# Recurrence of a hybrid transformer step: GpSimd's identity copy moved in the period, and three parts of the output weights instead of one among the last unit's steps

## What is computed

```python
def step(s, inp):
    r_t, w_t, k_t, v_t, z_t, b_t = inp
    sz = jnp.einsum('bhvk,bhk->bhv', s, z_t)
    s = s * w_t[:, :, None, :] + sz[..., None] * b_t[:, :, None, :] + v_t[..., None] * k_t[:, :, None, :]
    return s, jnp.einsum('bhvk,bhk->bhv', s, r_t)
...
o = ((o - mu) * lax.rsqrt(var + GN_EPS)).reshape(bsz, t_len, C_W)
o = o * lp['ln_g'] + lp['ln_b'] + (bonus_f + bonus_b).reshape(bsz, t_len, C_W)
g = jax.nn.sigmoid(xg) @ lp['g_lora']
return o * g, s_f, s_b
...
y = jnp.concatenate([y_a, y_b, y_c], axis=-1) @ lp['w_out']
x = x + g1 * y
```

## Time and profile before

| | |
|---|---|
| median of 3 runs | 2250.51 us (2247.64 to 2252.56) |
| profiled execution, its own time | 2250.14 us |
| its span on the core | 2248.3 us |
| mean granted TensorE clock | 0.968 |
| busy: PE, DVE, ACT, POOL | 93%, 47%, 33%, 7% |
| recurrence (start of its first period to ZU of the last unit) | about 635 to 955 us |
| output projection, block 0, parts 1 to 7 | 978 to 1008 us |

### The profile page before, as it was taken

How to read it: one execution, slowest core, us unless ns; L and a number is a source line. 1 busy time by engine, 2 the same in 40 slices (tenths; PEclk the granted TensorE clock), 3 DMA queues, 4 the chain that set the end, 5 groups by cost and what they waited for, 6 DMA issues and landing times.

```text
span 2248.3 us, 43915 instructions
## 1 busy us (share of the span) xinstructions
PE 2091.7 (93%) x19377; PEld 1834.2 (82%) x19377; DVE 1065.4 (47%) x1850; ACT 748.2 (33%) x1230; POOL 155.0 (7%) x248
## 2 busy tenths in 40 slices
PE   5899999999878888789799999999999999999997
PEld 2688888777657776678699999999999998887886
DVE  1432225554647777644554434444444444445444
ACT  2231222222454444422343233333232333333433
POOL 1000000000224433300000000000000000000000
PEclk8899999999889999989999999999999999999999
DMA  9888777775410010063343344334433446333441
GB/s 388 320 279 299 259 278 282 274 258 199 82 30 9 11 30 4 25 243 131 118 144 120 125 131 131 121 124 131 131 122 122 131 132 233 124 130 113 131 129 59
DMA packets 195999, 343.01 MB, mean 153 GB/s; under 512 B 14253, under 2 KB 137827, under 8 KB 193696
## 3 DMA queue, kind: packets, MB, share of 16 engines
q1 hardware_dynamic: 194416, 335.14, 43.8%
q0 software_dynamic: 1392, 5.05, 0.8%
HBM read 332.62 MB, written 10.31 MB: 153 GB/s over the span
## 4 chain that ended last, share of the span: by engine, by line
PE 81%; DVE 6%; POOL 4%; issue 4%; DMA 2%; ACT 2%; POOLq 0%; DVEq 0%; ACTq 0%; SPq 0%
PE ps L753 24%; PE ps L754 24%; PE ps L755 24%; PE ps L787 4%; DMA ring<-in_w_mod_dram 2%; POOL arena L716 1%; POOL ring L716 1%; POOL arena L733 1%; POOL w_mix L643 1%; POOL u_buf L732 1%; PE ps L985 0%; PE ps L995 0%; PE ps L977 0%; PE ps L979 0%; DVE h_split L1651 0%
## 5 line engine op out<-in xcount | busy, mean ns | idle before, releaser
L1589 DVE TENSOR_TENSOR w_split<-ring,w_split 128x1024 fp32r<-128x1024 f32 (+1 forms) x392 | 475.4, 1219 | 733.2 <-ACT w_split L1266 732.8
L1266 ACT ACTIVATE w_split<-ring 128x1024 fp32r<-128x1024 f32 (+1 forms) x392 | 407.0, 1051 | 827.5 <-PE ps L755 581.3
L753 PE MATMUL ps<-h_split,w_split 128*128 128x384 f32 x1776 | 599.3, 337 | 10.4 <-DVE w_split L1589 6.4
L755 PE MATMUL ps<-h_split,w_split 128*128 128x384 f32 x1776 | 595.9, 336 | 0.0
L754 PE MATMUL ps<-h_split,w_split 128*128 128x384 f32 x1776 | 595.9, 336 | 0.0
L753 PEld LDWEIGHTS ps<-h_split,w_split 128*128 128x128 f32 x1776 | 335.3, 189 | 23.8 <-issue 15.9
L754 PEld LDWEIGHTS ps<-h_split,w_split 128*128 128x128 f32 x1776 | 335.3, 189 | 0.0
L755 PEld LDWEIGHTS ps<-h_split,w_split 128*128 128x128 f32 x1776 | 335.2, 189 | 0.0
L753 PE MATMUL ps<-w_split,h_split 128*128 128x512 f32 (+1 forms) x528 | 199.5, 378 | 3.4 <-DVE w_split L1589 3.4
L754 PE MATMUL ps<-w_split,h_split 128*128 128x512 f32 (+1 forms) x528 | 196.4, 372 | 0.0
L755 PE MATMUL ps<-w_split,h_split 128*128 128x512 f32 (+1 forms) x528 | 196.3, 372 | 0.0
(11 more groups left out here) (373 smaller groups left out, 2623.6 us busy)
## 6 DMA issues: line engine op xcount, KB each, us to landing
ring<-in_w_mod_dram SPq DMA_DIRECT2D x96, 1024.0 KB, 8.1
ring<-in_w_up_dram SPq DMA_DIRECT2D x88, 1024.0 KB, 5.1
ring<-in_w_in_dram SPq DMA_DIRECT2D x46, 1024.0 KB, 5.6
ring<-in_w_down_dram SPq DMA_DIRECT2D x44, 1024.0 KB, 5.4
ring<-in_w_out_dram SPq DMA_DIRECT2D x16, 1024.0 KB, 5.2
arena<-in_x_sample_dram SPq DMA_DIRECT2D x4, 1024.0 KB, 14.3
x_mid<-arena SPq DMA_DIRECT2D x1, 3072.0 KB, 10.2
h_f<-x_mid SPq DMA_DIRECT2D x1, 3072.0 KB, 11.3
```

What stands on the lines that cost most here:

```text
L753: mm(o_, lh, rh, start=start, stop=False)
L755: return mm(o_, ll, rh, start=False, stop=stop)
L1266: AC(wh[k % SPLITS][:, 0:width(n)], arrived(n), ACT.Copy).then_inc(s_hi, 1)
L1589: V.tensor_tensor(wl[k % SPLITS][:, 0:w], arrived(n), wh[k % SPLITS][:, 0:w].bitcast(F32), ALU.subtract).then_inc(s_lo, 1)
```

## The change

It moves two steps, moves three rows of parameters, and takes parts 1 and 2 of the output projection's first block forward. TTp goes to the front of GpSimd's period, behind the square roots. eT becomes a step of its own behind X2's copy on ACT. Rows 9 to 11 of group 2 are loaded into `par[1]`, after group 1's last normalization. Parts 0 to 2 are split on ACT and DVE in periods 18 and 19, and their nine tiles are multiplied at fixed places among PE's steps.

```diff
-ORDER_ACT = ["ZU", "X0", "tanh", "X1", "eW", "exps", "X2", "X3", "out", "AV", "tr", "X4", "F2"]
+ORDER_ACT = ["ZU", "X0", "tanh", "X1", "eW", "exps", "X2", "eT", "X3", "out", "AV", "tr", "X4", "F2"]
-ORDER_POOL = ["F0", "kk", "k0", "bon", "Bb", "dP", "TTp"]
+ORDER_POOL = ["F0", "kk", "k0", "TTp", "bon", "Bb", "dP"]
...
+        def closing(gr):
+            return min(gr, 1)
...
+                    b = gr % 2 if i < 9 else closing(gr)
...
-                    for i in range(4):
+                    for i in range(3):
                         if i:
                             sp.wait_ge(s_rlora, NG + 3 + i)
                         params(2, range(3 * i, 3 * i + 3))
+                if gr == 1:
+                    sp.wait_ge(s_fy, 6)
+                    sp.wait_ge(s_fg, 6)
+                    params(2, range(9, 12))
...
-            def out_part(j, p):
+            def out_tile(j, p, t):
                 n = P_OUT + OUT_PARTS * j + p
                 pe.wait_ge(s_lo, rank(n) + 1)
...
+                if j == 0 and p == OUT_PARTS - 1:
+                    pe.wait_ge(s_fc, 3 * GROUPS)
...
+            early_tiles = {(NU, "QMms"): [(0, 0)], (NU, "S0"): [(0, 1)], (NU, "S1"): [(0, 2)], (NU, "F2"): [(1, 0), (1, 1), (1, 2)],
+                           (NU + 1, "F1"): [(2, 0)], (NU + 1, "F2"): [(2, 1), (2, 2)]}
             for u in PERIODS:
-                if u == NU + 1:
-                    pe.wait_ge(s_rdone, NU - 1)
-                    out_part(0, 0)
-                for step in steps(ORDER_PE, u):
-                    rwkv_step(u, *step)
-            pe.wait_ge(s_fc, 3 * GROUPS)
+                for step, v in steps(ORDER_PE, u):
+                    rwkv_step(u, step, v)
+                    for p, t in early_tiles.get((u, step), ()):
+                        if p == t == 0:
+                            pe.wait_ge(s_rdone, NU - 1)
+                        out_tile(0, p, t)
...
     ACT:
+                    if step == ("ZU", NU - 1):
+                        ac.wait_ge(s_rTu, LEVELS * NU)
+                        hi(P_OUT + 1)
+                        ac.wait_ge(s_rbp, NU)
+                        hi(P_OUT + 2)
...
-                if n == P_OUT + 1:
-                    ac.wait_ge(s_fc, 3 * GROUPS)
-                if n > P_OUT:
+                if n == P_OUT + 3:
+                    ac.wait_ge(s_fy, 3 * GROUPS)
+                if n > P_OUT + 2:
                     hi(n)
...
     DVE:
-                    if u == NU and step[0] == "F1a":
-                        lo(P_OUT)
+                    if (u, step[0]) in ((NU, "F1a"), (NU, "O"), (NU + 1, "F1a")):
+                        lo(P_OUT + ((NU, "F1a"), (NU, "O"), (NU + 1, "F1a")).index((u, step[0])))
```

More of the change, by code:

```diff
@@ L518, in params @@
             def params(gr, rows=range(12)):
-                cs, b = slice(HW * gr, HW * gr + HW), gr % 2
+                cs = slice(HW * gr, HW * gr + HW)
                 src = [a["rwkv_w0"][0, 0:1, cs], a["rwkv_w0"][0, 1:2, cs], a["rwkv_a0"][0, 0:1, cs], a["rwkv_a0"][0, 1:2, cs],
@@ L1140, in rwkv_step @@
                 elif step == "F1":
-                    pe.wait_ge(s_parf[pb], 16 * 3 * (gr // 2 + 1))
+                    pe.wait_ge(s_parf[closing(gr)], 16 * 3 * (1 + gr // 2))
                     if FINAL[v % NG][0]:
@@ L1146, in rwkv_step @@
                         pe.wait_ge(s_S0, 2 * gr + 2)
-                    mm(ps[:, 7, 0:HW], lora[:, 2, toks(FINAL[v % NG][1])], par[pb][:, 11, :], start=True, stop=True).then_inc(s_fg, 1)
+                    mm(ps[:, 7, 0:HW], lora[:, 2, toks(FINAL[v % NG][1])], par[closing(gr)][:, 11, :], start=True, stop=True).then_inc(s_fg, 1)
                 elif step == "F2":
@@ L1158, in out_part @@
                 w_hi, w_lo = parts(n, OUT_KQ)
-                for t in range(3):
[L1160 to L1166, removed]
-            for u in PERIODS:
-                if u == NU + 1:
-                    pe.wait_ge(s_rdone, NU - 1)
-                    out_part(0, 0)
-                for step in steps(ORDER_PE, u):
-                    rwkv_step(u, *step)
-            pe.wait_ge(s_fc, 3 * GROUPS)
+                if j >= 2 and p == 0:
+                    pe.wait_ge(s_oc, 3 * (j - 2) + t + 1)
+                if j == 0 and p == OUT_PARTS - 1:
+                    pe.wait_ge(s_fc, 3 * GROUPS)
+                for k in range(OUT_KQ):
+                    q = OUT_KQ * p + k
+                    last = three(ps[:, 3 * (j % 2) + t, 0:OUT_W], yh[:, q, toks(t)], yl[:, q, toks(t)],
+                                 w_hi[:, k, :], w_lo[:, k, :], start=(q == 0), stop=(q == KT - 1))
+                if t == 2:
+                    last.then_inc(s_blk, 1)
+            def out_part(j, p):
+                for t in range(3):
+                    out_tile(j, p, t)
+            early_tiles = {(NU, "QMms"): [(0, 0)], (NU, "S0"): [(0, 1)], (NU, "S1"): [(0, 2)], (NU, "F2"): [(1, 0), (1, 1), (1, 2)],
+                           (NU + 1, "F1"): [(2, 0)], (NU + 1, "F2"): [(2, 1), (2, 2)]}
+            for u in PERIODS:
+                for step, v in steps(ORDER_PE, u):
[4 more added lines that the diff above has]
+                        out_tile(0, p, t)
             pe.wait_ge(s_cyh, 1)
             for j in range(N_OUT):
-                for p in range(0 if j else 1, OUT_PARTS):
+                for p in range(0 if j else 3, OUT_PARTS):
                     out_part(j, p)
@@ L1421, in rwkv_step @@
                     AC(eN[z], ps[:, 2, 0:HW], ACT.Exp, scale=DECAY / 2, bias=expb[:, 4 + d:5 + d]).then_inc(s_rexp, 1)
+                elif step == "eT":
                     for c in range(2):
@@ L1940, in rwkv_step @@
                     elif step == "F1b":
-                        dv.wait_ge(s_parf[pb], 16 * 3 * (gr // 2 + 1))
-                        link(V.tensor_tensor(O, O, par[pb][:, 9, :], ALU.mult))
-                        link(V.tensor_tensor(O, O, par[pb][:, 10, :], ALU.add))
+                        dv.wait_ge(s_parf[closing(gr)], 16 * 3 * (1 + gr // 2))
+                        link(V.tensor_tensor(O, O, par[closing(gr)][:, 9, :], ALU.mult))
+                        link(V.tensor_tensor(O, O, par[closing(gr)][:, 10, :], ALU.add))
                         link(V.tensor_tensor(O, O, sq[1], ALU.add))
```

## The result

| | before | changed |
|---|---|---|
| median of the runs | 2248.21 us (5 runs, 2241.49 to 2252.56) | 2228.56 us (5 runs, 2225.95 to 2231.45) |
| profiled execution, its own time | 2250.14 us | 2228.56 us |
| its span | 2248.3 us | 2226.7 us |
| mean granted clock | 0.968 | 0.973 |

The ratio is 0.9914, with a 95% interval of 0.9899 to 0.9929: about 19.3 us less. The forecast was 2235.0 with a range of 2229.5 to 2243.5. The three runs before that the forecast started from were high: their median was 2250.51, that of the five runs here is 2248.21, and that of 18 runs beside the first experiments 2247.52.

A forecast was written before the change was run, and what follows sets the result against it. A chain of dependent steps was taken to bound the recurrence, and a full PE the projection from 982 on. Terms 8.8 - 0.1 + 6.7 = 15.4 us off 2250.14 gave 2235 us, range 2229.5 to 2243.5.

The forecast's parts named there:

- T0i's waits: Recurrence: GpSimd's identity copy ended twelve of 18 waits of T0i; moving it early leaves A as releaser, gaining 8.8 us.
- The forecast's sign: At T0i in the recurrence: all its waits would be released by PE line 1107 and none by the copy.
- so I charge nothing: Recurrence: the 0.40 us copy now runs where DVE works, but the square root still goes ahead of it; cost 0.
- eT and the start: ACT, first period: A(0) comes 1.9 us later, a table load (1.3) and part of X2's wait (0.5) go; +0.1 us.
- The handover: Recurrence to output projection: early tiles and splits remove PE's hole and the second low clock stretch; 6.7 us gained.
- +3.45: Handover: last transposes F2 start at 977.35 instead of 973.91, 3.45 us later on the chain.
- PE's instruction supply: Rival: unexplained PE gaps at fixed times eat the recurrence's gain, leaving 0 there; 2243.4 us, chance 0.10.
- The port decides: Rival: in seven normalization periods the copy meets DVE and costs its 0.40 us each, 2.8 us; 2237.5 us, chance 0.07.
- The clock stays low: Rival, handover: all nine tiles run at the low clock and parts 3 to 7 end 2 us later; 2243.4 us, chance 0.09.
- slower: Rival: low clock through the handover and on into parts 3 to 7; 2262 us with all 90 matmuls, chance 0.03.
- the copy was not the last: Rival: T0i's twelve waits were on A's matmuls all along, first term 0; above 2252 or 2249 us, chance 0.04.
- More than forecast: Rival, handover: the clock does not fall at 951.5 or rises by 962, up to 4 us more; 2231 us, chance 0.07.

The follow-up runs named there:

- E4: Changed kernel with the bonus's products back ahead of the identity copy on GpSimd, copy still ahead of Bb and dP; ratio 0.9944.
- E14: Same code as E4 again, side by side with the changed kernel; ratio 0.9930, median 2233.55 us.
- E12: Changed kernel with the identity copy ahead of the square root too, as GpSimd's first step of a period; ratio 0.9922, median 2230.05 us.
- E3: Changed kernel with the old GpSimd order and eT back ahead of X2's copy, so only handover and parameters changed; ratio 0.9962, 8.5 us less.
- E5: Changed kernel with the convolution's output back behind eT in the first period; ratio 0.9901.
- E11: The changed kernel measured once more, unaltered, in a later session; ratio 0.9916, median 2230.78 us.
- E1: Kernel before with one edit, GpSimd's identity copy moved ahead of the bonus; ratio 0.9964, 8.1 us less.
- E6: Changed kernel with all three tiles of part 0 behind S1, none before S0; ratio 0.9943.
- E8: Changed kernel with the convolution's output behind the copies of the first transposes on ACT; ratio 0.9887.
- E10: Changed kernel with part 0's first tile still before S0 and the other two behind S1; ratio 0.9929.
- E13: Same code as E8 again, beside the changed kernel on one chip; ratio 0.9895, median 2224.77 us.

## Why the prediction was right or wrong

- **T0i's waits** (8.8 us): the mechanism was right. The copy ends none of them any more, and the length of A's path is what they left. The twelve now start 0.10 to 0.11 us after A and not 0.05, so they gave 8.1 us. E4 and E14, with the copy early, eT moved and the bonus in its old place beside DVE, show it by itself: T0i(1) to T0i(17) takes 262.8 us as their mean and 271.0 in the two kernels with the old orders, 8.2 us. The forecast's sign, line 1107 as the releaser of all, is not what the view says: it gives line 1107 for five of the 18 and DVE's own line 1893 for the rest.
- **"so I charge nothing"** for the copy beside DVE: this step failed. The neighbour matters and the sign is opposite to the rival's: the copy didn't add 0.40 us, it took the place of a longer product. The rival spoke of it ("the copy would only take its place") and didn't price it. The saving is 0.35 us in seven periods at line 1939 (now 1961) and in two more at line 1788, 3.1 us in all (E4, E14, and E12 by its rows). With the waits that makes 11.2 us; the means of T0i(1) to T0i(17) are 271.0 us for the old orders (two profiles) and 259.9 for the changed code (seven), 11.1 apart. Line 1944, whose spread the forecast read for this, stands beside Bb's product (732), which the change left where it was; the line to read was 1939. The Trainium skill ("SBUF — State Buffer", section "SBUF: two separate sides") has the pair of ports locked for a whole instruction, and by that the order of the lengths was to be had in advance: the trace agrees in the order, with 0.27 and 0.28 us from GpSimd's end to DVE's. That is less than the 0.41 us that DVE's product takes alone.
- **eT and the start** (+0.1): wrong by a term. Where the clock's low stretches are alike it costs 0.8 to 0.9 us. The loss of A(0) was 3.0 us where 1.9 stood, because the copies of the transposes now start only after the second table load and eT. In the first pair of profiles it was hidden by the low stretch of 10 us in the kernel before.
- **The handover** (6.7): the mechanism was right, the term mis-sized: 8.4 us in the first pair of profiles and 8.5 us in E3 by its time. From F2(17) to part 8 it takes 23.8 us, which is 3.4 + 20.4 to the tenth; part 8's weights were split at 985.5, 1.3 us before PE wanted them (1.2 forecast), and PE did not wait. What was too large is F2(17) "+3.45": +2.46. S1 came +2.2 instead of +2.9, DVE's O step +2.0 instead of +2.75 and part 2's split cost 0.45 instead of 0.7. The clock had risen at 950.4, 25.8 us after T0i(17), where 27 stood; of the two cases between which 6.7 was taken, the quick one held (7.35), and the 1.0 us less of F2(17) makes 8.3 of it. DVE and PE in the changed kernel, which is the earlier trace rows after:

```profile
949.23 0.69 PE L1043 MATMUL ps<-w_mix,arena 64*64 64x64 f32 x8
...
951.68 0.45 PE L1043 MATMUL ps<-w_mix,arena 64*64 64x64 f32 x8
...
955.73 0.41 DVE L1890 TENSOR_TENSOR u_buf<-u_buf,ps 128x256 f32<-128x256 f32 x1
...
963.03 0.44 PE L1160 MATMUL ps<-consts,u_buf 128*128 128x128 f32 x2 [0.86 <-DVE u_buf L1968]
```

- **The sum**: waits 8.1, neighbours 3.1, the start -0.9, the handover 8.4: 18.7 us, against 19.3 and 18.9 by the ratios and 15.4 forecast. The term that was put at nothing, 3.1 us, is the largest part of the miss; the handover's 1.7 comes next, and the waits and the start take 1.5 back. The profiled pair differs by 21.6, 2.9 more: 1.8 of it goes with the low stretch at 658, and T0i(1) to T0i(17) in the changed kernel's profile (258.4) is 1.5 under the mean of its code, against 0.7 more ahead of the recurrence. That profile was lucky. The range reached 21 us below the old median, enough for the ratio, and missed the time because that median stood high.
- **The rivals**: "PE's instruction supply" falls. PE's unexplained gaps stay at their places in the program: in all 14 profiles one lies 5.9 to 6.7 us into period 9 and one 5.6 to 7.2 into period 15, 0.6 to 1.3 us each. Ahead of line 987 (979 before) they grew from 6.6 us to 7.2 (8), ahead of line 985 (977 before) they fell from 3.2 us (5) to 2.1 (5), so in sum they didn't grow:

```profile
  issue: 7.2, 8
```

"The port decides" had the right engines and the wrong sign. "The clock stays low" and "slower" fall with the windows, "the copy was not the last" with T0i, which moved up to A's end. "More than forecast" (2231) came nearest to the time, but not by its cause: in the profiled execution the clock rose 25.8 us after T0i(17), where its 962 means 24.0. It did rise before 24.0 in six others with this handover (E3, E5, E11 to E14), and T0i(17) to part 8 was there 60.6 to 61.5 us instead of 62.0 to 62.2, about 1 us and not 4.

## What to carry to other kernels

Take an idle engine's step that someone waits for to the front of its period; the gain is the wait down to the next releaser, read step by step. Where two engines start on one event and hold each other up, as GpSimd and DVE do here, the second is done only some 0.28 us after the first one's instruction: put a short one there. An order written for the steady state also decides the first period, where table loads fall between its steps; look at that period by itself.

## What the runs showed of the hardware that was not expected

The recurrence changes its length from run to run in steps. Period 5 took 18.2 to 18.3 us in the changed kernel and in E1, E5, E6 and E8, and 16.7 in E10, E11 and E13. The first five have a stretch at the lower clock level there and the last three have none. In the stretch PE is busy throughout, as it is at that place at full clock in E11. First the changed kernel, then E11, each with the 3 us ahead:

```profile
722.10:725.10 3.00, 1.55 (x71) 1.41 (x71) 2.93 (x9) 1.28 (x4) 0.90 (x2) 1.00 0.04 8
725.20:728.40 3.20, 3.20 (x86) 3.18 (x81) 1.76 (x5) 0.76 (x2) 1.34 (x3) 0.50 0.02 5
```

```profile
722.80:725.80 3.00, 1.54 (x69) 1.40 (x71) 2.93 (x9) 1.27 (x4) 0.90 (x2) 1.00 0.03 8
725.90:729.10 3.20, 3.20 (x111) 2.92 (x105) 1.76 (x5) 1.77 (x5) 1.34 (x3) 1.00 0.02 5
```

PE did the same ahead of both, and the clock fell in one. The stretch costs 1.5 us. E12 has one of 6.7 us in period 14 (19.2 us, where E4 and E14, without it, took 16.9), 2.3 us. PE is busy 6.36 of 6.70 us in it:

```profile
872.10:878.80 6.70, 6.36 (x136) 5.41 (x139) 6.02 (x17) 1.53 (x3) 1.89 (x3) 0.50 0.01 2
```

What decides whether such a stretch comes is open; no run here was made for it. That a stretch's 1.5 us is of the size of what one edit brings is the reason why E4, E6 and E12 had to be read by single periods.
